# Storing the convolution state of a hybrid decoder step: sixteen element-wise stores replaced by a transpose on TensorE and two stores of whole lines

## The reference

```python
def short_conv(x, left, w_in, conv_w, w_out):
    b_g, c_g, h = jnp.split(x @ w_in, 3, axis=-1)
    u = c_g * h
    u_ext = jnp.concatenate([left.astype(u.dtype), u], axis=1)
    z = conv_w[0] * u_ext[:, 0:s]
    for j in range(1, CONV_W):
        z = z + conv_w[j] * u_ext[:, j:j + s]
    return (b_g * z) @ w_out, u_ext[:, -(CONV_W - 1):]

def peer_ffn(x, w_q, keys, u_tab, v_tab):
    ...
    a = jnp.einsum('td,thkd->thk', xt, u_tab[idx])
    hk = g * jax.nn.gelu(a, approximate=False)
    return jnp.einsum('thk,thkd->td', hk, v_tab[idx])
```

## Time and profile before

| | us |
|---|---|
| median of 3 runs (lowest, highest) | 3518.87 (3518.16, 3523.32) |
| the profiled execution | 3523.25 |
| its span | 3521.2 |
| PE busy | 3059.3 (87%) |
| DVE busy | 2275.9 (65%) |
| ACT busy | 1171.7 (33%) |
| POOL busy | 1339.2 (38%) |

### The profile page before, as it was taken

How to read it: one execution, slowest core, us unless ns; L and a number is a source line. 1 busy time by engine, 2 the same in 40 slices (tenths; PEclk the granted TensorE clock), 3 DMA queues, 4 the chain that set the end, 5 groups by cost and what they waited for, 6 DMA issues and landing times.

```text
span 3521.2 us, 32961 instructions
## 1 busy us (share of the span) xinstructions
PE 3059.3 (87%) x9362; PEld 1708.0 (49%) x9362; DVE 2275.9 (65%) x5803; ACT 1171.7 (33%) x3492; POOL 1339.2 (38%) x1106
## 2 busy tenths in 40 slices
PE   8987679898988799999898899999996578888886
PEld 7744545444543356555553455655463244433333
DVE  0255667777557877778767767764675688777452
ACT  0014223233323443333333452322332244434331
POOL 0010034453434444434435334444544335445451
PEclk9998889999998899999999899999998799999998
DMA  4241189999999999999899899999999899999995
GB/s 185 96 156 48 60 341 421 378 421 380 421 420 421 384 411 415 421 421 404 349 420 422 339 401 378 416 410 409 421 420 243 319 379 370 409 379 398 421 421 219
DMA packets 179495, 1245.70 MB, mean 354 GB/s; under 512 B 20425, under 2 KB 24009, under 8 KB 31985
## 3 DMA queue, kind: packets, MB, share of 16 engines
q0 software_dynamic: 156160, 1111.70, 79.6%
q1 hardware_dynamic: 23008, 130.85, 9.4%
q10 hardware_dynamic: 144, 1.05, 0.1%
HBM read 1237.09 MB, written 6.46 MB: 353 GB/s over the span
## 4 chain that ended last, share of the span: by engine, by line
PE 51%; DVE 21%; DMA 15%; ACT 4%; issue 3%; DVEq 3%; another core or an unknown queue 2%; ACTq 1%; POOL 0%; POOLq 0%; SPq 0%
PE acc L1479 28%; DMA arena<-in_uv,idx 14%; DVE arena L1281 9%; PE bank L1504 8%; PE bank L1496 6%; PE bank L1317 3%; ACT diag L907 1%; ACT act_w L900 1%; PE bank L1344 1%; DVEq L1211 1%; PE bank L1390 1%; ACT L891 1%; DVE ya L1147 1%; DVE yb L1148 1%
## 5 line engine op out<-in xcount | busy, mean ns | idle before, releaser
L1479 PE MATMUL acc<-arena,diag 128*128 128x512 f32 x4160 | 1950.9, 625 | 333.3 <-ACT diag L907 331.8
L720 POOL DMA_INDIRECT arena<-in_uv,idx x1024 | 1280.2, 1250 | 1820.3 <-PE acc L1479 1533.7
L1281 DVE CUSTOM_DVE_ANT_0 arena<-arena,h 128x1024 f32<-128x1024 f32 x1024 | 1210.4, 1221 | 434.2 <-DMA arena<-in_uv,idx 432.6
L1479 PEld LDWEIGHTS acc<-arena,diag 128*128 128x128 f32 x4160 | 820.6, 200 | 1346.2 <-issue 948.3
L897 ACT ACTIVATE act_w<-dots 128x4 f32<-128x4 f32 x260 | 53.4, 205 | 1552.7 <-DVE dots L1281 1545.8
L1504 PE MATMUL bank<-hT,panel 128*128 128x256 f32 (+1 forms) x1792 | 408.3, 383 | 0.9 <-ACT hT L858 0.9
L1504 PEld LDWEIGHTS bank<-hT,panel 128*128 128x128 f32 x1792 | 338.5, 190 | 81.3 <-issue 34.5
L907 ACT ACTIVATE diag<-cst,act_w 128x128 f32<-128x128 f32 x1040 | 341.8, 391 | 96.0 <-PE acc L1479 77.0
L900 ACT ACTIVATE act_w<-act_w 128x1 f32<-128x1 f32 x1040 | 221.5, 283 | 22.0 <-issue 1.1
L1496 PE MATMUL bank<-panel,hT 128*128 128x256 f32 (+1 forms) x640 | 146.2, 383 | 2.7 <-DMA panel<-in_panels 1.8
L897 ACT ACT_TABLE_LOAD x109 | 139.8, 1283 | 1.1
(11 more groups left out here) (185 smaller groups left out, 2288.7 us busy)
## 6 DMA issues: line engine op xcount, KB each, us to landing
panel<-in_panels SPq DMA_DIRECT2D x109, 1024.0 KB
arena<-in_uv,idx POOLq DMA_INDIRECT x1024
arena<-in_cache_k POOLq DMA_DIRECT2D x16, 512.0 KB, 4.6
arena<-in_cache_v POOLq DMA_DIRECT2D x16, 512.0 KB, 4.5
lng<-in_ln SPq DMA_DIRECT2D x6, 512.0 KB
lnb<-in_ln SPq DMA_DIRECT2D x6, 512.0 KB
h<-in_h SPq DMA_DIRECT2D x1, 2048.0 KB
out_nv_p<-arena POOLq DMA_DIRECT2D x4, 512.0 KB, 10.4
```

What stands on the lines that cost most here:

```text
L720: nc.gpsimd.indirect_dma_start(uv[:, e % SLOTS_UV, :], None, uv_dram[layer], bass.IndirectOffsetOnAxis(ids[:, r:r + 1], 0)).then_inc(gathe ...
L1281: V.tensor_tensor_reduce(uv[:, e % SLOTS_UV, 0:D], uv[:, e % SLOTS_UV, 0:D], x_rows, 1.0, 0.0, ALU.mult, ALU.add, dots[:, G % 2, r:r + 1]) ...
L1479: m = mm(acc[:, half * 512:(half + 1) * 512], diag[:, r % DIAGS, :], uv[:, e % SLOTS_UV, D + half * 512:D + (half + 1) * 512], start=False ...
```

## The change

- `Plan.conv` adds, for g = 1 and after the last convolution piece, two pieces of a new kind `tails` (cost 1 each). For each, PE transposes four of the eight blocks of `tail`, 128 x 10 each, into the first ten partitions of a bank, and DVE copies these 10 x 512 values to `x_sample`. PE waits for `tail_ready` before them, which POOL waited for until now. After its copy DVE raises the new semaphore `tail_rows`.
- POOL waits for `tail_rows` to be 2 and stores rows 0 and 1 of `x_sample` to `cp`, rows 2 to 9 to `cs`, one DMA each, at the same place of its list.
- In layer 1, `x_spread` on DVE waits until both stores have landed (`conv_out` 32) before it overwrites `x_sample`. SP's wait at the end is for 32 too.
- The two pieces have bank numbers, so all later pieces use a bank two further on, and the pieces of the window in which they stand are spread anew.

```diff
 COST = {"mix": 8, "gate": 8, "conv": 8, "pq": 8, "proj": 2, "turn": 2, "norm_a": 4, "norm_b": 3, "route": 1,
-        "stage": 1, "side": 1, "i_spread": 1, "x_spread": 1}
+        "stage": 1, "side": 1, "i_spread": 1, "x_spread": 1, "tails": 1}
...
         out[0].fence = True
+        if g == 1:
+            out += [self.product(Piece("tails", half=i)) for i in range(2)]
         return out
...
-            sp.wait_ge(conv_out, 16 * 2 * C)
+            sp.wait_ge(conv_out, 32)
...
             pool.dma_start(cs[:, 0, :], state_conv[:, 1, :]).then_inc(conv_copy, 16)
-            pool.wait_ge(tail_ready, 1)
-            with nc.allow_non_contiguous_dma(reason="small state"):
-                for j in range(C):
-                    pool.dma_start(cp[:, j * P:(j + 1) * P].rearrange("s p -> p s"),
-                                   tail[:, j, 0:2]).then_inc(conv_out, 16)
-                    pool.dma_start(cs[:, 1, j * P:(j + 1) * P].rearrange("s p -> p s"),
-                                   tail[:, j, 2:2 + NS]).then_inc(conv_out, 16)
+            pool.wait_ge(tail_rows, 2)
+            pool.dma_start(cp, x_sample[0:2, :]).then_inc(conv_out, 16)
+            pool.dma_start(cs[:, 1, :], x_sample[2:2 + NS, :]).then_inc(conv_out, 16)
...
+                elif x.kind == "tails":
+
+                    dve.wait_ge(bank_full, n + 1)
+                    V.tensor_copy(x_sample[0:2 + NS, x.half * 512:(x.half + 1) * 512], bank[0:2 + NS, n % BANKS, :])
+                    dve.drain()
+                    dve.sem_inc(bank_free[n % BANKS], 1)
+                    dve.sem_inc(tail_rows, 1)
                 elif x.kind == "x_spread":
+                    if x.layer == 1:
+                        dve.wait_ge(conv_out, 32)
...
+                elif x.kind == "tails":
+                    pe.wait_ge(tail_ready, 1)
+                    for q in range(4):
+                        last = nc.tensor.transpose(bank[0:2 + NS, x.n % BANKS, q * P:(q + 1) * P],
+                                                   tail[:, 4 * x.half + q, :], const("ident"))
+                    last.then_inc(bank_full, 1)
```

More of the change, by code:

```diff
@@ L240, in sample_rows @@
         return [Piece("side", layer=layer)], \
-            [self.product(Piece("i_spread", layer=layer))] + [self.product(Piece("x_spread", half=i)) for i in range(2)]
+            [self.product(Piece("i_spread", layer=layer))] + [self.product(Piece("x_spread", layer=layer, half=i)) for i in range(2)]
     def next_layer(self, g):
@@ L569, in build @@
         tail_ready = sem("conv_state_ready")
+        tail_rows = sem("conv_state_rows")
         conv_out = sem("conv_state_stored")
```

## The result

The changed kernel takes 3468.06 us, median of four runs (3461.92 to 3469.20), beside 3520.28 us for the kernel before in its four. The ratio is 0.9847, with a 95% interval of 0.983 to 0.9865: 52 us less, 1.5%. The forecast was 3466.

The account below looks back on a forecast made before the run. DMA engines were taken to set the pace, clogged by single-element stores in slice 31. 55.7 - 0.5 - 1.5 = 53.7 us less gave 3469.6 from the profile, 3465.2 from the median; forecast 3466, own range 3457 to 3473, 8 in 10 3457 to 3480.

Parts of the forecast that it names:

- The stall belongs to the element stores: Layer 1, before expert 776's dot: sixteen element stores clog gathers; DVE waits 55.7 us over four dots, nearly all to go.
- The sum: Whole kernel: 55.7 less 0.5 less 1.5 gives 53.7 us saved.
- 0.5 us left: DVE's wait at the stores: 0.5 of 55.7 us stays, bounds 0 and 10.36.
- Transposes: PE, between last `conv` and first `mix` product: eight transposes of `tail` cost 1.5 us in full, lower bound 0.
- Copies on DVE: Two copies of 512 columns to `x_sample` cost 0 under a 5.31 us wait for PE; 1.3 us if uncovered.
- The pairs of `mix`: `mix` pieces of this window, paired at three places where two were: 0, bound by 3.62 us either way.
- The saving is kept: After the stall: DVE's work moves forward as a block, and the saving lasts to the end, where DMA sets the pace.
- Landing of the new stores: POOL's two whole-line stores: nearest like store landed 2.5 us after issue; the two hold 40 KB, 0.1 us at 421 GB/s.
- the rival that ends slower: Layer 1, `x_spread` waits for both stores; 0.2% slower only if one lands 317 us after issue; chance 0.02.
- The 4.4 us between the profile and the median: Profiled 3523.25 us against median 3518.87; unknown whether the 4.4 lies in the stall; forecast 3466 taken close to the median's.
- The price by the store: Rival at POOL's stores: fourteen fewer at 2.5 us, 35 less 1.5, gives 3485.4 us; chance 0.05.
- the estimate of 28 us: POOL's stores: fourteen fewer at a fixed cost of about 2.0 us each, giving about 3492 us.

Follow-up runs that it names:

- experiment 1: Kernel before without its sixteen stores of `tail`: 3470.2 us, 44.2 less than the kernel before on that chip (ratio 0.9875).
- experiment 7: Changed kernel with the sixteen element stores from `tail` in place of its two: 3516.5 us beside 3512.3 for the kernel before, ratio 1.0014.
- 11: Kernel before with its sixteen element stores moved behind the fourth head of tile 2, still on POOL: 3524.8 us, ratio 1.0022.
- Experiments 2 to 5: Kernel before with only `cp` stores 3476.5 us, only `cs` stores 3507.4, sixteen stores in longer runs 3466.0; changed kernel with sixteen whole-line stores 3467.9.
- `cs` alone: Kernel before with only the eight stores to `cs`, 8,192 single elements: 3507.4 us, 37.2 over the kernel with no stores.
- `cp` alone: Kernel before with only the eight stores to `cp`, 2,048 single elements: 3476.5 us, 6.2 over the kernel with no stores.

## Why the prediction was right, step by step

**The stall belongs to the element stores.** Right, and now shown both ways: without them it is gone (experiment 1), with all else of the change it stays (7), elsewhere it moves along (11).

**The sum.** 55.7 us of waiting were to go and 0.5 to stay. What went between the dots of 775 and 780 is 52.9 us (74.21 before, 21.33 after). The two numbers differ by the wait of 2.16 us for PE's key scores at 2706.78, by 0.41 and 0.20 us before dots, and by rounding. The term "0.5 us left" was the one of the wrong size: 2.8 is nearer. I had looked for what is late next among the gathers only; the next one late is PE, which restarts `acc` at this place. The gathers are there nearly in time, but not as worked out: by the trace's landings seven were still under way when the stores were issued, where I had counted four, and 776 to 779 landed from 2695.9 to 2703.4 instead of 2690.5 to 2698. The margin of 8 us that I saw for the first was 3.5, and the last was 0.41 late.

**Transposes.** Predicted 1.5 us in full, with 0 as a bound. Eight took 1.04 us on PE (beside 1.24 and 1.87 for the rows that I took), and the dots behind them came 0.9 us later, in the changed kernel as in experiment 7. By expert 775 that is swallowed: +2.40 us at 680 has become +0.60. DMA sets the pace from 2504 on, and it was in time.

**Copies on DVE.** Predicted at 0, under a wait of 5.31 us for PE. They took 0.68 us each, at 2369.88 and 2370.78, and the next dot started at 2371.71, 0.01 us from where it started before (2371.72), with the kernel 1.5 us behind at that time. Right.

**The pairs of `mix`.** Predicted at 0 with a bound of 3.62 either way. Expert 760 is at +0.12 us, 775 at +0.60. Right.

**The saving is kept.** -52.28 at 780, -53.63 at the last dot. Right; DVE in its own order, then DMA with the same bytes.

**Landing of the new stores.** I took 2.5 us from the store of the earlier trace rows. They landed after 13.7 and 16.1 us, since they stand behind seven gathers in POOL's queue, the last of which lands at 2693.1. Nobody waits for them: `x_spread` comes at 2935.64, 242 us later. The row was of a short queue: the store before it, of 512 KB, was issued 1.3 us earlier. The condition of the rival that ends slower was never near.

**The 4.4 us between the profile and the median.** The saving is 54.8 us between the two profiled executions and 52.2 between the medians of four, so some of the 4.4 may lie in the stall. That executions differ in the stall is shown (experiment 7); how much of the 4.4 it is stays open. That the forecast of 3466 is only 2 us off has some luck in it, since the kernels' executions are spread over 5 to 7 us.

**The price by the store** was the rival with 35 us. Experiments 2 to 5 rule it out. With it falls the estimate of 28 us from the fixed cost that the Trainium skill (DMA: Bandwidth & Descriptors, Anatomy of one DMA) gives for each DMA: it doesn't add up over stores in a row, of which sixteen took 3467.9 us where none took 3471.9. The other rule that the Trainium skill has (DMA: Bandwidth & Descriptors, Rules for kernel authors), one descriptor for each element of a last dimension that isn't contiguous, agrees with a price that goes by the elements.

**What stays open.** Where in the transfer the time goes isn't settled: with `cs` alone the stores' own packets are soon through, and the gathers' packets behind them are slow. Nor is it settled whether it is the reads of 4 bytes or the writes of 4 bytes; runs change both. Why 2,048 elements of `cp` cost 3.0 ns each and those of `cs` 4.5, and why runs of 8 and 32 bytes cost so little, is open too; 6 us are close to what these comparisons can tell, and between the dots of 760 and 780 `cp` alone costs 2.7. It wasn't tried at which length of run the price begins to fall.

## What to carry to other kernels

Look in the 40 slices for one in which the DMA engines are busy and GB/s is low, and ask which transfer in that queue names single elements. 40 KB in 10,240 elements cost 44 to 52 us of a kernel that lives on its transfers, 4 to 5 ns each, and the same 40 KB in sixteen stores of longer runs or whole lines cost nothing that could be seen; turn such data on an idle or covered engine first, and store whole lines. Moving them to SP's queue made it worse, and moving them to a stretch with little DMA work gives only a part back.

## What the runs showed of the hardware that was not expected

- The same sixteen stores cost more than twice as much on SP's queue (58 to 118 us over the kernel before, which already pays 44 on POOL's). Each element is a packet there, and packets of the two queues pass one to one, 3,341 of each in 140 us, at 173 GB/s in all. DVE waits 77 us longer for gathers than with no stores, 55 on POOL's queue, and 84.1 more for parameters that stand behind the elements in SP's list.
- On POOL's queue a store made 32 packets with 256 or with 1,024 elements in it, and the price still went with the elements: 6.2 us for 2,048, 37.2 for 8,192. With `cs` alone gathers were slow for some 40 us after the last of these packets had begun, and gathers issued ahead of the stores came up to 8.85 us late too.
- 2,048 runs of 8 and 32 bytes cost nothing to be seen (3466.0 us against 3470.2 with no stores), though 3.3 us of transfer was lost.
- A store of 32 KB landed 2.5 us after its issue behind one store of 512 KB, and 16.1 us behind seven gathers of 1 MB.
- In the stall of the kernel before, ACT and POOL waited for an unnamed releaser (18.7 and 14.8 us); in the kernel after there is no such wait in this stretch, and none in experiment 7 either, which has the stall. So the stall doesn't need it; what they waited for isn't shown.
